# Issuing expert weight transfers at the page ends of TensorE's instruction stream

## What is computed

```python
def moe_swiglu(h, router_w, w_gate, w_up, w_down):
    logits = (xt @ router_w).astype(jnp.float32)
    top_val, top_idx = lax.top_k(logits, TOP_K)          # TOP_K = 2 of 8
    gates = jax.nn.softmax(top_val, axis=-1)
    combine = jnp.einsum("nk,nke->ne", gates, jax.nn.one_hot(top_idx, N_EXPERTS))
    for e in range(N_EXPERTS):                            # w_gate, w_up: 1024 x 3584, w_down: 3584 x 1024
        y = y + combine[:, e:e + 1] * swiglu(xt, w_gate[e], w_up[e], w_down[e])
```

## Time and profile before

| | us |
|---|---|
| median of three runs | 1646.5 |
| lowest and highest run | 1637.96, 1648.85 |
| the profiled execution | 1640.96 |
| its span | 1639.1 |
| PE busy | 1525.7 |
| PEld busy | 1322.1 |
| DVE, ACT, POOL busy | 255.9, 178.8, 143.1 |

### The profile page before, as it was taken

The page is one execution under the profiler, slowest core; times in us unless marked ns, Lnnn a source line. Parts: engine busy times, 40 slices in busy tenths (PEclk is TensorE's granted clock), DMA queues, the critical chain, the costliest instruction groups (busy, mean ns, idle before and its releaser), DMA issues.

```text
span 1639.1 us, 53833 instructions
## 1 busy us (share of the span) xinstructions
PE 1525.7 (93%) x25789; PEld 1322.1 (81%) x25789; DVE 255.9 (16%) x473; ACT 178.8 (11%) x383; POOL 143.1 (9%) x167
## 2 busy tenths in 40 slices
PE   9999999999999999898998988998988899998997
PEld 8786587777677757898988888898888798888896
DVE  3333400000353433000100100100100100100102
ACT  4123210000322314000000000000000000000001
POOL 2243200000132423000000000000000000000000
PEclk9999999999999999999999999999999999999999
DMA  9204354444431357999999999999999999999970
GB/s 341 99 24 137 110 192 151 150 150 142 152 103 52 129 206 272 361 383 352 364 345 358 336 365 351 341 358 374 366 345 369 338 368 373 353 361 357 350 272 28
DMA packets 147656, 433.43 MB, mean 264 GB/s; under 512 B 9051, under 2 KB 33885, under 8 KB 147437
## 3 DMA queue, kind: packets, MB, share of 16 engines
q1 hardware_dynamic: 146432, 427.70, 71.4%
q0 software_dynamic: 672, 2.14, 0.5%
q10 hardware_dynamic: 332, 0.13, 0.0%
HBM read 428.89 MB, written 1.05 MB: 262 GB/s over the span
## 4 chain that ended last, share of the span: by engine, by line
PE 89%; issue 6%; DVE 2%; ACT 1%; POOL 1%; DMA 0%; ACTq 0%; DVEq 0%
PE ps L1040 34%; PE ps L1060 17%; PE ps L904 9%; PE ps L610 7%; PE ps L915 4%; PE ps L773 3%; PE ps L621 3%; PE ps L1084 2%; PE ps L980 1%; PE ps L730 1%; PE ps L740 1%; PE ps L636 1%; PE ps L643 1%; PE ps L606 1%; PE ps L750 1%
## 5 line engine op out<-in xcount | busy, mean ns | idle before, releaser
L1060 PE MATMUL ps<-LT_sb,ring 128*64 128x88 f32 x5376 | 217.2, 240 | 24.8 <-issue 24.1
L1040 PE MATMUL ps<-wpost,ring 128*64 128x88 f32 x5376 | 216.3, 240 | 21.5 <-issue 20.2
L1060 PEld LDWEIGHTS ps<-LT_sb,ring 128*64 128x64 f32 x5376 | 209.4, 137 | 33.3 <-issue 31.9
L1040 PE MATMUL ps<-AT_sb,ring 128*64 128x88 f32 x5376 | 214.8, 239 | 19.5 <-issue 19.3
L1040 PEld LDWEIGHTS ps<-wpost,ring 128*64 128x64 f32 x5376 | 209.0, 137 | 28.4 <-issue 26.7
L1040 PEld LDWEIGHTS ps<-AT_sb,ring 128*64 128x64 f32 x5376 | 208.1, 137 | 26.4 <-issue 26.2
L904 PEld LDWEIGHTS ps<-hT_sb,ring 128*128 128x128 f32 x768 | 136.0, 190 | 24.7 <-issue 9.1
L904 PE MATMUL ps<-hT_sb,ring 128*128 128x256 f32 (+1 forms) x768 | 155.7, 362 | 0.0
L610 PE MATMUL ps<-hT_sb,ring 128*128 128x256 f32 x592 | 131.7, 380 | 0.0
L610 PEld LDWEIGHTS ps<-hT_sb,ring 128*128 128x128 f32 x592 | 111.1, 190 | 15.4 <-DVE late L1504 0.5
L1838 POOL TENSOR_SCALAR small<-small 128x1 f32<-128x1 f32 x16 | 3.9, 241 | 1248.3 <-ACT late L1179 980.4
(11 more groups left out here) (280 smaller groups left out, 1102.4 us busy)
## 6 DMA issues: line engine op xcount, KB each, us to landing
ring<-in_moe_w_gate SPq DMA_DIRECT2D x84, 1024.0 KB, 7.1
ring<-in_moe_w_up SPq DMA_DIRECT2D x84, 1024.0 KB, 7.4
ring<-in_moe_w_down SPq DMA_DIRECT2D x84, 1024.0 KB, 7.5
late<-in_moe_w_up SPq DMA_DIRECT2D x28, 1024.0 KB, 7.3
late<-in_moe_w_gate SPq DMA_DIRECT2D x28, 1024.0 KB, 7.2
late<-in_moe_w_down SPq DMA_DIRECT2D x28, 1024.0 KB, 7.4
ring<-in_ffn_w_gate SPq DMA_DIRECT2D x11, 1024.0 KB, 5.4
ring<-in_ffn_w_up SPq DMA_DIRECT2D x11, 1024.0 KB, 8.0
```

The lines of the kernel that those rows point to most:

```text
L1040: ins = mm(o[lo:lo + P // 2, :], w[:, i, m * P + lo:m * P + lo + P // 2], xgT[e % 2][:, k, :], start=(k == 0 and m % 4 == 0), stop=(k == K ...
L1060: ins = mm(o[lo:lo + P // 2, :], d[:, i, m * P + lo:m * P + lo + P // 2], moe_hid[:, 2 * j + i, :], start=(first and m % 4 == 0), stop=las ...
```

## The change

The new table counts PE's instructions through the expert stage, in pages of 256, and names a matmul some 16 instructions before each page's end (`PAGE_TURNS`). That matmul also increments a new semaphore, `page_turn`. For each unit, `UNIT_TURN` gives the number of the first such signal behind the unit's last matmul. In the first round SP issues unit n only when unit n - 16 is used and that signal has come. Sizes, order, buffers and the other engines' programs are as they were.

```diff
+PAGE = 256
+FIRST_IN_PAGE = 67
+PAGE_LEAD = 16
+UNIT_CALLS = 32
+WAITS = {"g0": 5, "u0": 1, "g1": 2, "d0": 2, "u1": 1, "g2": 2, "gather": 2, "d1": 1, "u2": 1, "g3": 2, "d2": 1,
+         "u3": 1, "d3": 1, "y": 2, "s0": 1, "s1": 0, "oh": 0}
...
+def page_turns():
+
+    at, turn_at, turns, unit_turn = FIRST_IN_PAGE - WAITS["g0"], PAGE - PAGE_LEAD, set(), []
+    for e in range(N_EXP):
+        for owner, name, calls, size, signal_every in pe_order(e):
+            at += WAITS[name]
+            for i in range(calls):
+                at += size
+                has_signal = i % signal_every == signal_every - 1
+                if has_signal and signal_every == UNIT_CALLS:
+                    unit_turn.append(len(turns) + 1)
+                if at >= turn_at and not has_signal:
+                    turns.add((owner, name, i))
+                    turn_at += PAGE
+    return turns, unit_turn
...
                     if first and n < N_UNIT:
                         first_free(n)
+                    elif first:
+                        sp_.wait_ge(unit_used, n - N_UNIT + 1)
+                        sp_.wait_ge(page_turn, UNIT_TURN[n - N_UNIT])
                     else:
...
+            def turned(ins, e, block, call):
+                if (e, block, call) in PAGE_TURNS:
+                    ins.then_inc(page_turn, 1)
...
                                 ins = mm(o[lo:lo + P // 2, :], w[:, i, m * P + lo:m * P + lo + P // 2],
                                          xgT[e % 2][:, k, :], start=(k == 0 and m % 4 == 0), stop=(k == KD - 1),
                                          skip_group_check=True)
+                                turned(ins, e, f"{kind}{c}", call)
+                                call += 1
```

More of the change, by code:

```diff
@@ L98, with pe_order, tiles, once @@
 ROUND_UNITS = len(UNITS)
+PAGE = 256
[4 more added lines that the diff above has]
+         "u3": 1, "d3": 1, "y": 2, "s0": 1, "s1": 0, "oh": 0}
+def pe_order(e):
+    def tiles(kind, owner, c):
+        return owner, f"{kind}{c}", UNIT_CALLS * (MOE_TILES[c] // 2), 4, UNIT_CALLS
+    def once(flag, *block):
+        return [block] if flag else []
+    more = e < N_EXP - 1
+    return ([tiles("g", e, 0)] + ([tiles("d", e - 1, MOE_CH - 1)] if e else [(0, "oh", 2, 2, 2)])
+            + [tiles("u", e, 0)] + once(e, e - 1, "y", 8, 2, 8) + [tiles("g", e, 1)] + once(e, e - 1, "s0", 2, 4, 2)
+            + [tiles("d", e, 0)] + once(e, e - 1, "s1", 2, 4, 2) + [tiles("u", e, 1), tiles("g", e, 2)]
+            + once(more, e + 1, "gather", 48, 2, 24) + [tiles("d", e, 1)] + once(more, e + 1, "oh", 2, 2, 2)
+            + [tiles("u", e, 2), tiles("g", e, 3), tiles("d", e, 2), tiles("u", e, 3)])
+def page_turns():
[12 more added lines that the diff above has]
+    return turns, unit_turn
+PAGE_TURNS, UNIT_TURN = page_turns()
 assert ROUND_UNITS % N_UNIT == 0
@@ L345, in build @@
         yT_act, yT_dve, yT_ps = (sem(n) for n in ("yT_act", "yT_dve", "yT_ps"))
+        page_turn = sem("page_turn")
         moe_acc = [sem(f"moe_acc{t}") for t in range(TT)]
@@ L1006, in gather @@
                     pe.wait_ge(ohT_ready, per_round(r, 1, N_EXP))
+                call = 0
                 for k in range(KD):
@@ L1010, in gather @@
                             ins = gather_part(j, k, t, n, t == 0 and n == 0, t == 1 and n == 2)
+                            turned(ins, e, "gather", call)
+                            call += 1
                     if k % 4 == 3:
@@ L1018, in onehot_transposes @@
                     ins = mm(bank(6)[0:SLOTS, t * P:(t + 1) * P], onehot[e % 2][:, t, :], ident_bf, start=True, stop=True)
+                    turned(ins, e, "oh", t)
                 ins.then_inc(ohT_ps, 1)
@@ L1062, in m_down @@
                                          skip_group_check=True)
+                                turned(ins, e, f"d{c}", call)
+                                call += 1
                     ins.then_inc(unit_used, 1)
@@ L1072, in y_transposes @@
                     ins = nc.tensor.transpose(bank(6 + m // 4)[0:SLOTS, m % 4 * P:(m % 4 + 1) * P], yT[:, m, :], ident)
+                    turned(ins, e, "y", m)
                 ins.then_inc(yT_ps, 1)
@@ L1085, in scatter @@
                              y_tok[:, half * 512:(half + 1) * 512], start=True, stop=True)
+                    turned(ins, e, f"s{t}", half)
                 ins.then_inc(scatter_ps, 1)
```

## The result

The changed kernel takes 1699.3 us (median of four runs, 1691.05 to 1707.98) against 1647.7 us of the kernel before (four runs): a ratio of 1.032, 95% interval 1.028 to 1.037. The forecast was 1770 us. The direction was right, and the loss is 52 us (50 between the profiled executions) where some 130 were forecast.

A forecast was written before the change was run, and what follows sets the result against it. Bound by nearly full DMA engines and PE, whose idle time is late instruction fetches. A mean stall of 1.43 us over 164 pages gave 234 us against 101, +133: 1774, taken as 1770 us, range 1600 to 1860.

The forecast's parts named there:

- Fetches every 256 instructions, late because of queued weights: Expert stage: PE fetches pages of 256 instructions, delayed behind queued weight units; some 101 us of idle time.
- The signal, the increments, the release at the page's end: Increments cost PE 0 us; SP sees the signal at the page's end and issues both units 0.4 us apart.
- signs a and b of the forecast: SP issues one pair a page, 0.4 to 0.5 us apart; PE's gaps stay every 128 loads, neighbours adding up to 4.5.
- Good and bad pages: Per expert of 21.4 pages: 8 good, request before the pair, 0.05 us stall; 13.4 bad, pair ahead.
- What a bad page costs: At a bad page's end the fetch waits for both units whole; mean stall 2.25 us.
- the next stall is 6.9 - w + 2.45 - 4.85 = 4.5 - w: In bad pages, w is PE's stall at this page's end; two neighbouring stalls add up to 4.5 us.
- My reading of the stall at 827.26: Longest stall before the change: the fetch started 5.6 us behind its request, read as two units' worth.
- Rival 3: At page ends the fetch waits for one unit, not two: 0.95 us mean stall, +55 us, 1696 us; chance 0.10.
- 3.2 us or more: In stalled pages before the change, how long the fetch starts behind the last one's arrival.
- 1.35 us: Best case behind a stall before the change: PE goes on at 1076.34, the next fetch starts 1.35 us later.
- Rival 1: At page ends the request stays ahead of the pair: 0.35 us of stall a page, 1597 us; chance 0.15.
- The other signs: Profile after the change: larger issue waits, lower DMA rate with dry patches, later fetches, no PE wait on a weight tile.

The follow-up runs named there:

- e5: The kernel before, with each unit behind the first 16 bringing only its first half, with as many issues: 1530.7 us, a single run.
- e1: The changed kernel with PE's increments kept but SP's wait for them taken out: 1646.2 us, ratio 1.003 to the kernel before.
- e9: The changed kernel with the signal on the page's end instead of 16 instructions before it: 1633.4 us, ratio 0.990 to the kernel before.
- e7: The changed kernel with each unit sent as two DMAs of half its rows: 1694.2 us, ratio 1.030 to the kernel before.
- e6: The changed kernel with the signal 8 instructions behind the page's end instead of 16 before it: 1603.0 us, ratio 0.974 to the kernel before.
- e12: The changed kernel with the signal 4 instructions behind the page's end instead of 16 before it: 1605.3 us, ratio 0.978 to the kernel before.

## Why the prediction was right in kind and wrong in size

*Fetches every 256 instructions, late because of queued weights:* right. The fetches are in the earlier trace rows, and e5 shows what makes them late (half the data, hardly a stall).

*The signal, the increments, the release at the page's end:* right. PE's increments cost nothing that can be told (e1), the pair goes out 0.46 us apart at the end (signs a and b of the forecast). The table's count was off by some 3 instructions, as I had read it; e9 shows that this is enough to matter when the signal lies on the end.

*Good and bad pages:* right in kind. In bad pages the pair is ahead of the request (96% of the stalls); behind a scatter there are two or three good ones. I took 13.4 bad of 21.4, which is 103 over the stage; measured are 116.

*What a bad page costs:* **the step that failed.** "So a fetch goes behind every unit issued up to its request, whole": I read this from the fetches at 1008.16 and 819.22, which did start as a unit ended. In the kernel before, SP's issues are mostly 2.4 us apart or more, and what is ahead of a request is mostly out before it has waited that long, so only a third of its stalls (33 of 105) cut into a unit, and I had not looked at those. In the changed kernel nearly all do (100 of 116): the fetch starts 3.9 us behind X in the median, 3.5 to 4.5 in 80% of the cases, and 3.8 (3.1 to 4.7) with four units issued. The bound is not sharp, since single waits reach 5.4 us. So "the next stall is 6.9 - w + 2.45 - 4.85 = 4.5 - w" should read 3.9 + 2.45 - 4.85 = 1.5 us, whatever w was, and neighbours don't add up to 4.5. The term was mis-sized at 2.25 us; measured is 1.28 in the mean, since the first stalls of a run are small. 116 x 1.28 = 148 us against 106 in the same count of the kernel before: +42 us, of a span that is 50 us longer. The sum had +133.

My reading of the stall at 827.26 was half right. The 5.6 us are about two units' worth, but the units were not whole: by the count of the last column this fetch, too, cut into a unit. The unit issued at 816.85 landed at 823.95 and that of 819.27 by 826.4 (7.1 us behind its issue as well), while that of 821.70 landed only at 831.0, so the data right ahead of the fetch was a part of this last one. The evidence against the third rival stands, and "whole" does not. At 5.6 us behind my reckoned request this wait is also longer than that of any stall above, so either I set the request too early or the bound gives way here; the record does not say which.

Two smaller readings were off. "3.2 us or more" for a stalled page was one stall's number (in the kernel before F - X is 3.4 us in the median, 2.1 to 4.1), and 1.35 us was not the best case: behind the stall that ends at 1533.07 the fetch starts after 1.05 us. Nothing in the sum hung on either.

*Rival 3* gave 1696 us, 3 from the measured. Its time was near by luck, not by its mechanism: it has the fetch wait for one transfer, start 4.3 us behind the pair's first issue and stall for 0.95 us in every page. Measured are 5.3 us, stalls of 1.28 in 116 pages and none in the rest, and halved transfers (e7) leave it as it was. What it had right is that a fetch need not wait for both units whole.

*Rival 1*, the pair behind the request, is what e6 and e12 make true on purpose: it gave 1597 us, they take 1603 and 1605. Its reason is shown; in the changed kernel it isn't so.

*The other signs:* issue before weight loads was forecast at 200 us or more and is 154.5; single gaps at 2 to 3 us, and the longest is 2.2; the rate at 310 GB/s and is 341; the fetch at 4 to 5 us behind PE's going on and behind both units, and it is at 3.9 and inside the second; the dry patches are there. PE's wait on a weight tile, which would have shown the 16 units too few, grew nowhere.

*Still open:* whether the bound is one of bytes (66 to 75 KB a DMA engine) or of time, why single waits exceed it, and the last 8 us of the span.

## What to carry to other kernels

PE, which here needs 256 instructions every 4.85 us, fetches them through the same DMA engines as the data; idle time put down to "issue" at every 128th matmul was this. Issue large transfers just behind the page's end, not just ahead of it: here 24 instructions (0.5 us) were the difference between 3.2% lost and 2.6% gained. And before a wait is costed from "it goes behind all that is queued", look for the case in the trace in which much is queued, since a bound shows only there.

## What was new about the hardware

With two 1 MB units issued ahead of its request, an instruction fetch starts about 3.9 us behind it (PE's going on taken as the request; 10 to 90%: 3.5 to 4.5), and much the same with four units (3.8; 3.1 to 4.7), with half transfers (3.8; 3.3 to 4.4) and in pieces of 2 KB (3.9; 3.3 to 4.5); single waits reach 5.4 us. The earliest fetch behind a stall of the kernel before started after 1.05 us (the stall that ends at 1533.07). From the start of a fetch it takes 2.45 us until PE goes on.
